# Splitting the wide part of an f32 score product into three f32r passes in one layer of a four-layer decoder

## The reference, cut to what matters

```
def step(carry, xs):
    ...
    w_intra = jnp.exp(logw - m_t[..., None])
    w_inter = jnp.exp(log_inter - m_t)
    a = jnp.einsum('bhtd,bhsd->bhts', qx, kx, preferred_element_type=jnp.float32) * w_intra
    num = (jnp.einsum('bhts,bhsv->bhtv', a, vx)
           + w_inter[..., None] * jnp.einsum('bhvd,bhtd->bhtv', C, qx))
```

## Time and profile before

| | |
|---|---|
| Time, median of 3 runs | 1760.14 us (1760.11 to 1761.57) |
| Time of the profiled execution | 1759.14 us |
| Its span, first to last instruction | 1757.4 us |
| Granted TensorE clock, mean | 0.999 of full speed |
| Busy: TensorE matmul, VectorE, ScalarE | 99%, 65%, 52% |
| Chain of work that ended last | 98% TensorE matmul |
| DMA, mean over the span | 178 GB/s |

### The profile page before, as it was taken

The page is one execution under the profiler, slowest core; times in us unless marked ns, Lnnn a source line. Parts: engine busy times, 40 slices in busy tenths (PEclk is TensorE's granted clock), DMA queues, the critical chain, the costliest instruction groups (busy, mean ns, idle before and its releaser), DMA issues.

```text
span 1757.4 us, 25060 instructions
## 1 busy us (share of the span) xinstructions
PE 1747.9 (99%) x8278; PEld 1459.6 (83%) x8278; DVE 1142.0 (65%) x1900; ACT 908.9 (52%) x1420; POOL 38.0 (2%) x99
## 2 busy tenths in 40 slices
PE   9999999999999999999999999999999999999998
PEld 7888888888888888888888888888888888888887
DVE  6766766665658888855656455655666666666655
ACT  7454545454546666655544445444545445454543
POOL 1000000000000000000000000000000000000000
PEclk9999999999999999999999999999999999999999
DMA  8565565555565554556997699855565656556564
GB/s 252 179 188 177 171 188 166 181 174 184 186 189 165 156 154 140 172 179 165 161 165 200 186 162 181 212 173 190 181 184 163 182 178 182 177 179 179 167 215 144
DMA packets 171012, 313.16 MB, mean 178 GB/s; under 512 B 10838, under 2 KB 27804, under 8 KB 170812
## 3 DMA queue, kind: packets, MB, share of 16 engines
q1 hardware_dynamic: 170512, 311.02, 62.9%
q10 hardware_dynamic: 380, 1.08, 0.2%
q0 software_dynamic: 48, 0.13, 0.1%
HBM read 310.10 MB, written 2.10 MB: 178 GB/s over the span
## 4 chain that ended last, share of the span: by engine, by line
PE 98%; issue 1%; DVE 0%; ACT 0%; DMA 0%; SPq 0%; POOLq 0%; POOL 0%; DVEq 0%; ACTq 0%
PE acc L944 30%; PE acc L946 30%; PE acc L945 30%; PE tp L909 4%; PE sc L945 1%; PE sc L946 1%; PE sc L944 1%; PE sc L976 0%; DMA xres<-in_x_dram 0%; PE sc L1030 0%; PE sc L1032 0%; ACT w_hi L881 0%; PE sc L1031 0%; PE sc L1014 0%; PE sc L1013 0%
## 5 line engine op out<-in xcount | busy, mean ns | idle before, releaser
L1755 DVE TENSOR_TENSOR w_lo<-raw,w_hi 128x1024 fp32r<-128x1024 f32 x583 | 708.2, 1223 | 468.1 <-ACT w_hi L881 466.9
L881 ACT ACTIVATE w_hi<-raw 128x1024 fp32r<-128x1024 f32 x583 | 613.4, 1058 | 467.4 <-PE acc L946 415.2
L944 PE MATMUL acc<-w_hi,xt_hi 128*128 128x512 f32 x1824 | 720.5, 395 | 0.0
L946 PE MATMUL acc<-w_hi,xt_lo 128*128 128x512 f32 x1824 | 711.8, 390 | 0.0
L945 PE MATMUL acc<-w_lo,xt_hi 128*128 128x512 f32 x1824 | 710.6, 390 | 0.0
L946 PEld LDWEIGHTS acc<-w_hi,xt_lo 128*128 128x128 f32 x1824 | 342.6, 188 | 73.0
L945 PEld LDWEIGHTS acc<-w_lo,xt_hi 128*128 128x128 f32 x1824 | 343.2, 188 | 65.9
L944 PEld LDWEIGHTS acc<-w_hi,xt_hi 128*128 128x128 f32 x1824 | 342.9, 188 | 65.5
L944 PE MATMUL acc<-w_hi,ot_hi 128*128 128x512 f32 (+1 forms) x520 | 202.7, 390 | 0.0
L946 PE MATMUL acc<-w_hi,ot_lo 128*128 128x512 f32 (+1 forms) x520 | 201.0, 387 | 0.0
L945 PE MATMUL acc<-w_lo,ot_hi 128*128 128x512 f32 (+1 forms) x520 | 200.6, 386 | 0.0
(11 more groups left out here) (286 smaller groups left out, 1136.3 us busy)
## 6 DMA issues: line engine op xcount, KB each, us to landing
raw<-in_da_w_in_dram SPq DMA_DIRECT2D x255, 512.0 KB, 3.8
raw<-in_ml_w_in_dram SPq DMA_DIRECT2D x96, 512.0 KB, 5.4
raw<-in_sw_w_in_dram SPq DMA_DIRECT2D x72, 512.0 KB, 3.8
raw<-in_da_w_out_dram SPq DMA_DIRECT2D x64, 512.0 KB, 4.3
raw<-in_sw_w_out_dram SPq DMA_DIRECT2D x32, 512.0 KB, 4.0
raw<-in_ml_w_in_dram SPq DMA_DIRECT2D x64, 256.0 KB, 4.7
raw<-in_ml_w_out_dram SPq DMA_DIRECT2D x32, 512.0 KB, 4.6
xres<-in_x_dram SPq DMA_DIRECT2D x3, 512.0 KB, 10.0
```

The source lines that it names most:

```text
L881: act.activation(w_hi[:, q:q + 2, :], raw[:, q:q + 2, :], ACT.Copy).then_inc(hi_ready, 1)
L944: pe.matmul(out_ap, k_hi, m_hi, start=start, stop=False)
L946: return pe.matmul(out_ap, k_lo, m_hi, start=False, stop=stop)
L1755: dve.tensor_tensor(w_lo[:, q:q + 2, :], raw[:, q:q + 2, :], w_hi[:, q:q + 2, :].bitcast(F32), ALU.subtract).then_inc(lo_ready, 1)
```

## The change

The score product of the third layer is rewritten. The part with 256 columns becomes a call of `three` on split copies, and the part with 128 columns stays a plain f32 matmul on whole copies. The whole copies now hold only queries 128 to 255 and keys 128 to 255. No new buffers are made: the split q uses `kT_hi` and `kT_lo`, the split k uses `q1_hi` and `q1_lo`, all four idle in this layer. Both banks are now read by ACT and by DVE, and DVE frees them. The semaphore `qk_hi` counts the two hi copies of an iteration.

```
-    "qk_hi":     ((0, 0, 0), (0, 4, 0), (0, 0, 0), (0, 0, 0)),
+    "qk_hi":     ((0, 0, 0), (0, 4, 0), (0, 0, 0), (0, 2, 0)),
...
-        qT, kT = (a[:].rearrange("p (h t) n -> p h (t n)", t=T) for a in (q0, k0))
+        ml_q1, ml_k1 = q0, k0
+        ml_q_hi, ml_q_lo, ml_k0_hi, ml_k0_lo = kT_hi, kT_lo, q1_hi, q1_lo
...  (ACT, place 19)
-                    take(qT[:, 0:2, :], "tp_0", tp[0][:], in_iter(l, "tp_0", i, 0))
+                    act.wait_ge(full["tp_0"], in_iter(l, "tp_0", i, 1))
+                    act.activation(ml_q_hi[:, 0:2, :], turned(0), ACT.Copy).then_inc(sig["qk_hi"], 1)
+                    act.wait_ge(full["tp_1"], in_iter(l, "tp_1", i, 1))
+                    act.activation(ml_k0_hi[:, 0:2, :], turned(1)[:, :, 0:P], ACT.Copy).then_inc(sig["qk_hi"], 1)
...  (TensorE, places 17 and 18)
-                        pe.matmul(sc[h][:, 0:S], kT[:, h, 0:P], qT[:, h, :], start=True, stop=True)
-                        pe.matmul(sc[h][:, S:BLK], kT[:, h, P:S], qT[:, h, P:S], start=True, stop=True)\
+                        three(sc[h][:, 0:S], ml_k0_hi[:, h, :], ml_k0_lo[:, h, :], ml_q_hi[:, h, :], ml_q_lo[:, h, :], True, True)
+                        pe.matmul(sc[h][:, S:BLK], ml_k1[:, h, :], ml_q1[:, h, :], start=True, stop=True)\
                           .then_inc(full[f"sc_{h}"], 1)
...  (DVE, place 19)
-                    take(kT[:, 0:2, :], "tp_1", tp[1][:], in_iter(l, "tp_1", i, 0))
+                    for b, (whole, hi, lo, cols) in enumerate(((ml_q1, ml_q_hi, ml_q_lo, slice(0, S)),
+                                                               (ml_k1, ml_k0_hi, ml_k0_lo, slice(0, P)))):
+                        dve.wait_ge(full[f"tp_{b}"], in_iter(l, f"tp_{b}", i, 1))
+                        dve.wait_ge(sig["qk_hi"], in_iter(l, "qk_hi", i, b + 1))
+                        dve.tensor_copy(whole[:, 0:2, :], turned(b)[:, :, P:S])
+                        dve.tensor_tensor(lo[:, 0:2, :], turned(b)[:, :, cols], hi[:, 0:2, :].bitcast(F32), ALU.subtract)\
+                           .then_inc(free[f"tp_{b}"], 1)
```

## The result

The changed kernel takes 1762.30 us (median of 22 runs, 1760.84 to 1764.15) against 1760.10 us for the kernel before (22 runs, 1758.63 to 1761.57). The ratio is 1.0014, with a 95% interval of 1.0008 to 1.0020. It is 2.2 us slower where I forecast 0.5 us faster. Its profiled execution has a span of 1761.7 us, 4.3 more than before.

A forecast was written before the change was run, and what follows sets the result against it. TensorE's own stream, busy 99%, was taken as the bound. The passes' -0.64 us plus 0.1 us of waiting gave -0.54, taking the median of 1760.14 to 1759.6 us (chance 0.65), range 1758.6 to 1761.3 us.

The forecast's parts named there:

- The passes, -0.64 us: Third layer's score product: three f32r passes replace the 256-column f32 matmul, 0.08 us less on each of eight heads.
- The tail: Ten slower 512-column steps on TensorE behind a score product, 2.31 us instead of 2.264; expected to stay, 0.046 us a head.
- rival (a): The slower steps behind the third layer's score product vanish too: gain 1.1 us, 1759.0 us; chance 0.12.
- rival (b): Weight loads stand in TensorE's stream; a fifth 0.188 us load per head makes it 0.9 us slower, 1761.0; chance 0.03.
- DVE's delay, 0.98 us plus 0.6 where it had been idle: DVE's score copies and subtracts make it 0.98 to 1.25 us later, some 0.6 more waiting for ACT's first copy.
- The wait there, +0.1 us: Third iteration of the third layer: TensorE may wait 0 to 0.2 us for w_lo of pair 19; 0.1 put in.
- the one on the load: SP loads pair 23 later by 1 to 1.6 us; TensorE wants it four pairs on, over 10 us later.
- cover: Third iteration: new copies end 0.8 us before the scores; margin for w_lo of pair 19 goes from 1.2 to 0.2–0 us.
- Rival (c): TensorE waits in the third layer for w_lo of pair 19: 0.6 us slower, all four iterations 4.2; chance 0.15.
- The range: 1758.6 to 1761.3 us: the spread of the three runs of before, 1.5 us, said to be laid about the forecast.

The follow-up runs named there:

- The held load: The kernel before with the third layer's load of pair 23 issued after w_lo of pair 20 instead of 19: 1760.62 against 1759.26 us.
- the load brought forward: The changed kernel with the v accumulator emptied at place 20 instead of 19, so load 23 goes out earlier: 1759.36 against 1759.80 us.
- the later transposes: Third layer's transposes of place 35 at 36, copies behind at 40; on the changed kernel 1758.29 against 1759.26 us, on a third chip 1758.98 against 1759.43.
- the control: The kernel before with the transposes of place 35 at 36, copies behind at 40: 1758.81 against 1759.80 us, on a third chip 1758.73 against 1759.43.
- the passes alone: The kernel before with only the three f32r passes on TensorE, on ready operands, ACT and DVE copying as before: 1758.71 against 1759.26 us.

## Why the prediction was wrong

- **The passes, -0.64 us: right in the trace,** 1.04 us instead of 1.12 from one matmul to the second behind, and in size by the times, -0.55, -0.53, -0.61 and -1.00 us where no late load took it back. The first two intervals reach zero, so the trace is the better evidence. The tail stayed (2.31 us), so rival (a) falls. Passes 0.12 us apart are far from three loads of 0.188 end to end, so the rule on weight loads that the Trainium skill gives in "TensorE: Matmul & The Clock Gate", section "Part 3: Packing small matmuls", does not hold for these shapes, and rival (b) falls with it.
- **DVE's delay, 0.98 us plus 0.6 where it had been idle: right.** 1.55 us in the first iteration, counted from the transposes. The whole delay reached w_lo of pair 19, as said. **The wait there, +0.1 us: right,** in the third iteration, 0.10 us. By their groups DVE's four operations take 7.8 us against 2.8, as forecast, and ACT's copies 3.9 against 2.4; the busy times of the page rise by only 3.0 and 0.1 us, since it counts overlapping records once.
- **The step that failed** is the one on the load: "The later w_lo also lets SP load pair 23 later by 1 to 1.6 us; it is wanted by TensorE four pairs on". The size was right (1.38 us), but I costed it at nothing by the distance to its own use. Here the load went out late into an idle queue that was full from there on, and the time was taken from all the loads behind it. I read the DMA's 178 GB/s and its share as means over the span, and not for the third layer, where behind that load the share is 1.02. The held load shows that this step alone costs 1.36 us, and the load brought forward takes 2.1 us off the changed kernel.
- **The margin of the other consumers was not read.** From three listed waits, none in the third layer, I concluded that nothing there was close to one, and looked for cover only at the two places next to the change, the scores and pair 19. The place without margin was the transposes of place 35, 16 pairs further on, with 0.05 us of wait already in the profiled execution and 0.7 to 1.0 us by what the later transposes brought to the kernel before. Rival (c) had TensorE waiting for DVE, but for w_lo of pair 19, at a price of the delay less the margin. At that place only the 0.1 us came; the loss took another path, by the loads, which no rival had.
- **The half clock behind a wait was not in any sum.** It is 1.6 us in the profile and 1.9 between the two kinds of runs.
- **The range** did not follow from its own words. The three runs of before lie from 0.03 below to 1.43 above their median, which laid about 1759.6 gives 1759.6 to 1761.0, not 1758.6 to 1761.3. The measured 1762.30 is outside either.

Not settled: how 1.38 us of lost queue become 1.85 at the mix, beyond the spread of 1.1 us that this mix has between profiles without a late load; and why it is the first and the third iteration that have no margin. The loads of the next iteration's first job are halves of 256 KB and come slower, but no run changed them.

## What to carry to other kernels

Where work is added to an engine that frees buffers for loads, ask what the transfer queue is doing at the moment of the freeing, in that layer: if it is idle there and full afterwards, as here, the delay can go to everything that the queue carries until it is full no longer, and show at the consumer with the least margin, here 50 us on. So read the DMA share in windows around the change, and read margins from start to start of the bound engine, not from the list of waits. An engine that is 99% busy can have next to no margin at one instruction of a loop, here in two of its four iterations (0 and 0.2 us), and making it faster uses up margin as well. And where a fix is tried on the changed kernel, try it on the kernel before too: the later transposes looked as if they had kept the gain, until the control had gained as much.

## What the runs showed that I had not expected

In two profiles of the changed kernel TensorE stood four times before the transposes of place 35. Behind 2.48 and 2.29 us from start to start it then worked for 3.2 us at a granted clock of 0.50, its lower level of 1.2 GHz; behind 2.12 and 2.06 us it did not. The fall costs more than half of the wait again. It seems to separate the runs of one kernel into two groups 1.9 us apart. And a stream of 512-column matmuls is slower for some nine steps (2.31 us for ten instead of 2.264, and 2.29 to 2.30 with the passes alone) behind a short f32 matmul that stands last, whatever stands before it; behind the three f32r passes that stand last in layer 0 it is not (nine steps in 2.04 us). I have no cause for it.
